# A two-network transformer kernel on one core: weight ring, upper halves and arena put one behind the other at multiples of 4096 bytes

## The reference, cut to what matters

```python
for l in range(DEPTH):                      # first network, 2 layers
    proj = rms_norm(x, attn_norm[l]) @ w_in[l]
    ...                                     # three branches, gated and merged
    x = x + merged @ w_out[l]
    h2 = rms_norm(x, mlp_norm[l])
    x = x + jnp.square(jax.nn.relu(h2 @ w_up[l])) @ w_down[l]
for i in range(DEPTH_2):                    # second network, 4 layers
    y = mixer[i](x * (1.0 + scale1) + shift1)
    x = layer_norm(DN_ALPHA * x + (1.0 + gate1) * y, ...)
    u = causal_dwconv((x * (1.0 + scale2) + shift2) @ w_up[i], conv_w, conv_b)
    gate, val = jnp.split(u, 2, axis=-1)
    x = layer_norm(DN_ALPHA * x + (1.0 + gate2) * ((silu(gate) * val) @ w_down[i]), ...)
```

## The kernel before

| tensor | bytes | start | start modulo 4096 |
| --- | --- | --- | --- |
| ring | 49,152 | 2,176 | 2,176 (= 17 x 128) |
| upper | 16,384 | 51,328 | 2,176 |
| x | 8,192 | 67,712 | 2,176 |
| cols (parameters) | 7,856 | 75,904 | 2,176 |
| const | 12,856 | 83,776 | 1,856 (= 29 x 64) |
| ada_sum | 4,096 | 97,408 | 3,200 |
| stat | 8,192 | 102,208 | 3,904 |
| arena | 114,688 | 112,448 | 1,856 |

## Time and profile before

### The profile page before, as it was taken

The page is one execution under the profiler, slowest core; times in us unless marked ns, Lnnn a source line. Parts: engine busy times, 40 slices in busy tenths (PEclk is TensorE's granted clock), DMA queues, the critical chain, the costliest instruction groups (busy, mean ns, idle before and its releaser), DMA issues. The chain is left out here.

```text
span 2624.4 us, 46404 instructions
## 1 busy us (share of the span) xinstructions
PE 2446.8 (93%) x18912; PEld 2318.6 (88%) x18912; DVE 1946.6 (74%) x3284; ACT 1388.1 (53%) x2545; POOL 12.9 (0%) x20
## 2 busy tenths in 40 slices
PE   7899999988999999889998979999988999998998
PEld 6699999977999999879998879997788999976998
DVE  5477788754877886788887778886458889856884
ACT  6444555355455543646644556746463674434663
POOL 0000000000000000000000000000000000000000
PEclk8799999988999999989999999999989999988999
DMA  5124567721155678304565624573334457632552
GB/s 219 48 97 147 213 244 288 303 107 65 65 193 193 228 290 304 125 35 147 191 257 224 241 89 159 195 298 113 144 129 147 159 194 289 258 114 77 193 181 93
DMA packets 64084, 462.89 MB, mean 176 GB/s; under 512 B 7232, under 2 KB 7424, under 8 KB 8064
## 3 DMA queue, kind: packets, MB, share of 16 engines
q1 hardware_dynamic: 63872, 459.92, 47.5%
HBM read 458.85 MB, written 1.05 MB: 175 GB/s over the span
## 5 line engine op out<-in xcount | busy, mean ns | idle before, releaser
L770 PE MATMUL psum<-arena_rounded,upper_rounded 128*128 128x256 f32 (+2 forms) x5112 | 1450.9, 284 | 94.7 <-PEq L659 27.9
L771 PE MATMUL psum<-arena_rounded,upper_rounded 128*128 128x256 f32 (+2 forms) x5112 | 1437.4, 281 | 0.0
L772 PE MATMUL psum<-arena_rounded,ring_rounded 128*128 128x256 f32 (+2 forms) x5112 | 1436.8, 281 | 0.0
L770 PEld LDWEIGHTS psum<-arena_rounded,upper_rounded 128*128 128x128 f32 (+2 forms) x5112 | 972.1, 190 | 114.5 <-issue 62.7
L569 DVE TENSOR_TENSOR ring_rounded<-ring,upper_rounded 128x1024 fp32r<-128x1024 f32 (+4 forms) x958 | 840.0, 897 | 311.0 <-ACT upper_rounded L560 306.1
L560 ACT ACTIVATE upper_rounded<-ring 128x1024 fp32r<-128x1024 f32 (+4 forms) x958 | 751.6, 795 | 567.9 <-PE psum L772 483.5
L771 PEld LDWEIGHTS psum<-arena_rounded,upper_rounded 128*128 128x128 f32 (+2 forms) x5112 | 973.8, 190 | 0.7 <-issue 0.5
L772 PEld LDWEIGHTS psum<-arena_rounded,ring_rounded 128*128 128x128 f32 (+2 forms) x5112 | 972.3, 190 | 0.1
L591 DVE SCALAR_TENSOR_TENSOR ada_sum<-ring,small,ada_sum 128x1024 f32<-128x1024 f32 x168 | 214.9, 1279 | 1.3
L2369 DVE SCALAR_TENSOR_TENSOR arena<-psum,cols,arena 128x255 f32<-128x255 f32 (+1 forms) x352 | 153.3, 478 | 64.6 <-ACT arena L2336 61.5
L2336 ACT ACTIVATE arena<-psum,cols 128x256 f32<-128x256 f32 x176 | 89.5, 561 | 76.1 <-PE psum L772 76.0
(11 more groups left out here) (499 smaller groups left out, 2453.3 us busy)
## 6 DMA issues: line engine op xcount, KB each, us to landing
ring<-stream_dram SPq DMA_DIRECT2D x434, 1024.0 KB, 4.9
const<-const_dram SPq DMA_DIRECT2D x1, 1540.0 KB, 14.2
x<-x_dram SPq DMA_DIRECT2D x1, 1024.0 KB, 4.9
out_dram<-x SPq DMA_DIRECT2D x4, 256.0 KB, 2.1
cols<-cols_dram SPq DMA_DIRECT2D x1, 978.0 KB, 11.0
const<-const_dram SPq DMA_DIRECT2D x1, 67.0 KB, 4.6
pos<-positions_dram SPq DMA_DIRECT2D x1, 64.0 KB, 5.4
cols<-cols_dram SPq DMA_DIRECT2D x1, 4.0 KB, 4.4
```

The source lines that it names most:

```text
L770: pe.matmul(out, upper, x[0][:, b.k, :], start=(b.k == 0), stop=False)
L771: pe.matmul(out, upper, x[1][:, b.k, :], start=False, stop=False)
L772: ins = pe.matmul(out, lower, x[0][:, b.k, :], start=False, stop=(b.k == nk - 1))
```

## The change

Three edits in the constructor: a filler tensor brings the first free byte to a multiple of 4096 before `ring` is allocated, `arena` is allocated directly behind `upper`, and the small tensors follow behind it.

```diff
+        def begin_at_multiple_of(edge, rest=0):
+
+            gap = (rest - (nc.sbuf_base + 31) // 32 * 32) % edge // 4
+            if gap:
+                sb(f"gap_{nc.sbuf_base}", gap)
+
...
+        begin_at_multiple_of(4096)
         self.ring = sb_rounded_too("ring", RING * UNIT)
         self.upper = sb_rounded_too("upper", CHUNKS * CHUNK)
+        self.arena = sb_rounded_too("arena", ARENA, ARENA_CUTS)
         self.x = sb("x", KD * T)
...
         self.cos, self.pos = sb("cos", T), sb("pos", T, I32)
-        self.arena = sb_rounded_too("arena", ARENA, ARENA_CUTS)
```

## The result

The changed kernel takes 2667.39 us (median of 4 runs, 2665.22 to 2668.52) against 2616.32 us: the ratio is 1.0194, with a 95% interval of 1.0176 to 1.0211. It is slower by 51 us, 36 us above the upper end of the predicted range.

What follows compares the result with a forecast made beforehand. TensorE was taken as the bound, busy 2446.8 of 2624.4 us, mostly with the three split products. Four terms of 0 on the median gave 2616.77 + 0, written 2616 us; the 8-in-10 range was 2599 to 2631.

Steps and rivals of the forecast that it cites:

- The two values of the step: TensorE's time from one matmul to the next in stretches without idle time: 113.1 ns (short) or 117.6 ns (long).
- Part 1: TensorE's split products reading ring, upper and arena at other bytes: change of the step taken as 0.
- upper end for a loss: TensorE's split products: if every short step became a long one, at most 15,216 x 4.5 ns = 68 us lost.
- Part 2: VectorE's and ScalarE's operations on the moved tensors: cost taken as 0, L569 staying at 1222 and L560 at 1055 ns.
- Part 3: DMA landings in the ring: taken as 0, ends 54.7 us either way; aligned-start rule worth 1.7 us, left out.
- fall below 47.5%: Sign for the DMA aligned-start rule: the stream's packets taking less than 47.5% of the engines.
- Part 4: The 480-column filler and the new order, with small tensors and constants moved: no instruction, cost 0.
- The draw: Which step follows a stop of TensorE: mostly the same again; if drawn anew, 4.8 us per wide product either way.
- rival B: Faster: long-step stretches get the short step, 9.5 us for first and fourth wide products, 2607 (further 2600); chance 0.22.
- C: Slower: equal remainders make weight and activation reads clash; second and third wide products get the long step, 9.5 us, 2626; chance 0.18.
- D: Larger gain: aligned starts take cycles out of both steps, 2 ns x 15,216 = 30 us, 2586; chance 0.05.
- E: Alignment changes nothing because a 32- or 64-byte granule matters, which every tensor already had; 2617; chance 0.05.

Runs made afterwards that it cites:

- e3: The changed kernel with 64 bytes of filler ahead of the arena; 2632.54 us, 1.0050 of the kernel before.
- e1: The changed kernel without the filler ahead of ring, so ring, upper and arena all lie 2,176 past a multiple of 4096; 2667.73 us.
- e2: The kernel before plus the filler ahead of ring (ring at 4,096), arena still last; 2616.91 us against 2618.21 before.
- e4: The changed kernel without the filler ahead of ring, with 704 bytes ahead of the arena; 2618.93 us against 2618.21 before.
- e13: The changed kernel without the filler ahead of ring, with 448 bytes ahead of the arena; 2620.01 us against 2620.05 before.
- e17: The kernel before with 128 bytes of filler ahead of upper and nothing else; 2584.63 us, 0.9863 of the kernel before.
- e15: The changed kernel with fillers that put upper at 128 and arena at 192 modulo 4096, ring at 0; 2647.16 us.
- e16: The changed kernel without the filler ahead of ring, with upper 2304 and arena 2496 past a multiple of 4096; 2586.04 us.
- e14: The changed kernel with a filler that puts upper and arena at 192 modulo 4096, ring at 0; 2643.04 us.
- e9: The changed kernel with fillers that put upper at 64 and arena at 256 modulo 4096, ring at 0; 2657.48 us.
- e12: The changed kernel with 96 bytes of filler ahead of the arena; 2671.35 us, 1.0199 of the kernel before.

## Why the prediction was wrong

**What bounds the kernel.** Right: the end moved with TensorE's step (50.4 us of busy time); of the rest only the idle time moved, by 9.5 us the other way. The two values of the step and their difference of 4.5 ns were read rightly too.

**Part 1, the step that failed.** "Four sources and one price for each form: I take 0 for the change of the step." It measured +3.7 ns on 14,870 steps, +55 us. The rows used as bounds were of other forms, and of the distance they vary little or nothing. The one-column product reads its weights in `ada_sum` and its column in `const`. These two lie 13,632 bytes apart before and after, and in every kernel here, so its 0.111 and 0.113 us say nothing on distance. One such product of 96 rows did have its distance changed, from 0 to 64 modulo 256 (L1294, weights in the arena), and its 64 matmuls take 14.0 us both times. In L2217 the weights are in `const` and the activation in the arena: their distance went from 0 to 64 too, and its matmuls still start 215.8 ns apart. For the split products the same two distances are 119.9 and 117.1 ns (e3), so these forms do not carry over. They bounded nothing for L770 to L772, and no row has these at another distance. The prediction's upper end for a loss, every short step a long one, had no step longer than both; 120.0 ns is that step.

The deeper fault stands a paragraph higher: "the places read before and after are the same sort of places", from which I concluded that data's place has no part in the step. Every place in ring and upper is a multiple of 512 bytes from the tensor's start and nearly every activation tile a multiple of 1024. Modulo 256 all of them are one and the same place. The trace held the variable that counts fixed at 192, and I took its constancy for a lack of effect.

**What sets the step.** Shown: it is where weights and activation lie to each other modulo 256, not the alignment to 4096 (e1, e2), not the order or the far distance (e4, e13, e17). Moving all three tensors by 128 modulo 256 changes nothing (the changed kernel and e1, before and e2). A move of all three by less was not tried: the ring begins at 0 or 128 modulo 256 in every kernel. The distance of ring and upper from each other is no cause by itself, as it is 128 in both e15 (118.0 ns) and e16 (113.6 ns). Shown also: it is a matter of how loads and matmuls follow each other, as the distance of ring's loads and that of upper's act together (e14, e15, e16) and the steps fall into repeating patterns (e9, e12). With 192/192 or 64/64 there are two patterns, and after a stop either may follow; with 0/0 there is one, the slow one; with 64/192 one, the fast one.

No other engine is needed for it. In the changed kernel's trace 671 of the counted steps fall where neither VectorE nor ScalarE works, and their mean is 119.8 ns; in 237 of them no DMA packet is under way either, with the same mean. One such stretch (by its count, 25 matmuls in 2.70 us, the edges taken in; its starts lie 119.8 ns apart):

```profile
2267.80:2270.50 2.70, 2.70 (x25) 2.70 (x24) 0.00 (x0) 0.00 (x0) 0.00 (x0) 1.00 0.69 291
```

What is left are TensorE's own two streams. That the weight load and the matmul beside it read SBUF at the same time and get in each other's way there is the explanation that I hold likely. e9's 290 against 283 ns speaks for it; e14 does not follow from it simply, e15 has its long step beside a load at distance 192, and it isn't proven. What happens in which cycle stays open.

The Trainium skill ("TensorE: Matmul & The Clock Gate", section "Part 2: What happens when you issue a matmul") says that TensorE has two independent SBUF read ports, and that the next weights' load takes no read bandwidth from the running matmul. No run here shows the ports. The same loads and the same matmuls take 113.5 or 119.9 ns by their addresses; the measurement decides.

**Part 2.** Right: 1221 ns against 1222, 1055 against 1055.

**Part 3.** Right: waits for the ring's landing 54.7 us both times. The prediction also weighed a rule of the Trainium skill ("DMA: Bandwidth & Descriptors", section "How a descriptor splits into AXI transactions"), which is worded for what a transaction reads, while the ring's start is where the packets are written. By it, as an estimate, packets should be 1.5% cheaper in a ring at 4,096 (changed kernel) than at 2,176 (e1, else the same distances). The packets of 8192 bytes take 309 ns in the median and 352 and 351 ns on average in these two traces, so the rule does not show. The queue's share did fall below 47.5%, the sign that the prediction had named for it, but e1 has the same 46.4%. The longer span alone would give 46.8%.

**Part 4.** Right for the filler by itself (e2: 0.9993).

**The draw.** I called an anew-made draw unlikely by three runs 1.6 us apart. On other chips and at other times the kernel before has run from 2606.7 to 2629.6 us, so the draw is most likely made in each execution; there is one trace of each kernel, so no two executions of the same one can be held side by side. The traces of before and e4, both at 192/192, can: before has long steps in two wide products and e4 in none, their counted steps differ by 12.5 us in sum, and their times by 11.9 us (2626.14 and 2614.28). So the profiled execution of before wasn't long for its profile, it had mostly drawn long steps. The changed kernel's was 2667.12 us with a median of 2667.39, and there one step leaves nothing to draw. The terms of rival B and C, 4.8 us for a wide product, were the right size for it.

**The rivals.** C came nearest, with equal remainders of weights and activation as the cause, and it had the sign. It failed in size: it put the loss at 9.5 us, the long old step in two stretches, where a third, longer step took all of them. And equal remainders are not the whole law, as 96 bytes cost the same. Its chance was held down by VectorE's full speed at equal remainders, a row of another engine that could not speak for TensorE's reads. B had the right thought that some relative positions of the bytes let the long step in and others don't: at 64/192 it is gone (e16, e17; 34 and 35 us less), at a position that this change does not take. D, with steps below both old ones, is seen nowhere; that its 30 us are near e16's 34 is chance. E is refuted: 64 bytes were not the grain.

## What to carry to other kernels

Where TensorE is the bound and its loads and matmuls run back to back, the byte addresses of weights and activations are a parameter of the kernel: try fillers of 32 to 224 bytes ahead of one of the tensors, measure each, and read the step as length over matmuls in a stretch without idle time. Two values of that step for the same code are the sign to look for. When a trace shows no effect of something, ask first whether the trace varies it: count in the unit that could matter, here bytes modulo 256. And change one address relation at a time; a round number is a distance of zero to every other round number.

## What the runs showed of the hardware

- The split product with 256 columns has steps of 113.3, 117.8 and 120.0 ns at a granted clock of 1.00, besides mixed patterns, by the distance of its two reads modulo 256 bytes; the best and the worst layout take 2584.63 and 2671.35 us, 3.4% of this kernel.
- Equal remainders are bad (119.9 ns), but 96 bytes are as bad (119.9), 32 (116.8) are better than 128 (118.9), and 64 for one tensor with 192 for the other is better than either for both.
- It holds with VectorE and ScalarE idle (119.8 ns over 671 steps of the changed kernel).
- An unsplit float32 product with 256 columns has the same 215.8 ns at distances 0 and 64, and a product of 96 rows that streams one column the same 14.0 us for 64. No other distance was tried on these forms.
- Layouts with two patterns in their trace had widely spread executions (2606.7 to 2629.6 us for the one before in 65 of them, 2632.0 to 2649.4 for e15 in seven); layouts with one pattern are 3 to 4 us wide (2665.2 to 2668.5 and 2581.4 to 2585.2 us, four executions each). A spread can be a property of the layout, not of the measurement.
